# Feed-forward gate and up columns in six pairs of 488, 472, 488, 472, 456 and 440, with the activation made in place

## The reference

```
D_FF = 2816
h = RMSNorm(x)                                 # 256 x 1024
gate, up = split(h @ w_up)                     # w_up is 1024 x 5632: 2816 gate columns, 2816 up columns
x = x + (silu(gate) * up) @ w_down             # w_down is 2816 x 1024
```

## Time and profile before

| | us |
|---|---|
| median of 3 runs | 861.86 (861.78 to 861.89) |
| span of the profiled execution | 859.8 |
| PE busy | 855.7 |
| DVE busy | 593.9 |
| ACT busy | 446.0 |
| POOL busy | 113.6 |

### The profile page before, as it was taken

How to read it: one execution, slowest core, us unless ns; L and a number is a source line. 1 busy time by engine, 2 the same in 40 slices (tenths; PEclk the granted TensorE clock), 3 DMA queues, 4 the chain that set the end, 5 groups by cost and what they waited for, 6 DMA issues and landing times.

```text
span 859.8 us, 11140 instructions
## 1 busy us (share of the span) xinstructions
PE 855.7 (100%) x4246; PEld 711.6 (83%) x4246; DVE 593.9 (69%) x850; ACT 446.0 (52%) x646; POOL 113.6 (13%) x89
## 2 busy tenths in 40 slices
PE   9999999999999999999999999999999999999998
PEld 7888888888888888888888888888888888888887
DVE  7896967768777665564479768768696765565543
ACT  7567654854454444443364674558443644444431
POOL 0750101005401000000005401010063000000000
PEclk9999999999999999999999999999999999999999
DMA  9846656475657666555566465665665576665641
GB/s 343 290 150 190 200 175 183 148 228 180 188 184 236 190 195 190 182 185 189 162 186 178 119 195 158 196 197 162 205 196 179 151 234 183 185 190 177 195 147 50
DMA packets 87815, 160.53 MB, mean 187 GB/s; under 512 B 7505, under 2 KB 14161, under 8 KB 87761
## 3 DMA queue, kind: packets, MB, share of 16 engines
q1 hardware_dynamic: 87328, 159.16, 58.8%
q10 hardware_dynamic: 432, 0.66, 0.2%
HBM read 158.74 MB, written 1.05 MB: 186 GB/s over the span
## 4 chain that ended last, share of the span: by engine, by line
PE 93%; DVE 3%; DMA 2%; ACT 1%; SPq 1%; issue 0%; ACTq 0%
PE bulk L1692 28%; PE bulk L1696 28%; PE bulk L1693 28%; DMA raw<-in_w_in_dram 2%; DVE w_lo L1013 2%; PE bankAB L1432 1%; PE bankAB L1634 1%; PE bankT L1587 0%; PE bankAB L1576 0%; ACT w_hi L737 0%; PE bankAB L1441 0%; PE bankAB L1532 0%; PE bankO L1545 0%; PE bankT L1634 0%; PE bankO L1634 0%
## 5 line engine op out<-in xcount | busy, mean ns | idle before, releaser
L1013 DVE TENSOR_TENSOR w_lo<-raw,w_hi 128x1024 fp32r<-128x1024 f32 (+1 forms) x288 | 362.3, 1272 | 156.5 <-ACT w_hi L737 152.9
L737 ACT ACTIVATE w_hi<-raw 128x1024 fp32r<-128x1024 f32 (+1 forms) x286 | 297.7, 1049 | 245.3 <-PE bulk L1696 240.8
L1692 PE MATMUL bulk<-w_hi,hT_hi 128*128 128x512 f32 (+1 forms) x880 | 344.1, 391 | 0.2 <-DVE w_lo L1013 0.2
L1693 PE MATMUL bulk<-w_lo,hT_hi 128*128 128x512 f32 (+1 forms) x880 | 339.2, 385 | 0.0
L1696 PE MATMUL bulk<-w_hi,hT_lo 128*128 128x512 f32 (+1 forms) x880 | 336.5, 386 | 0.0
L1692 PEld LDWEIGHTS bulk<-w_hi,hT_hi 128*128 128x128 f32 x880 | 165.3, 188 | 33.2 <-DVE w_lo L1013 0.7
L1696 PEld LDWEIGHTS bulk<-w_hi,hT_lo 128*128 128x128 f32 x880 | 165.0, 188 | 33.4
L1693 PEld LDWEIGHTS bulk<-w_lo,hT_hi 128*128 128x128 f32 x880 | 165.4, 188 | 31.7
L1692 PE MATMUL bulk<-w_hi,aT_hi 128*128 128x512 f32 x174 | 68.0, 391 | 0.0
L1696 PE MATMUL bulk<-w_hi,aT_lo 128*128 128x512 f32 x174 | 67.7, 389 | 0.0
L1693 PE MATMUL bulk<-w_lo,aT_hi 128*128 128x512 f32 x174 | 67.7, 389 | 0.0
(11 more groups left out here) (259 smaller groups left out, 720.7 us busy)
## 6 DMA issues: line engine op xcount, KB each, us to landing
raw<-in_w_in_dram SPq DMA_DIRECT2D x110, 512.0 KB, 4.1
raw<-in_w_ffn_up_dram SPq DMA_DIRECT2D x80, 512.0 KB, 4.4
raw<-in_w_ffn_down_dram SPq DMA_DIRECT2D x44, 512.0 KB, 3.3
raw<-in_w_branch_dram SPq DMA_DIRECT2D x20, 512.0 KB, 4.2
raw<-in_w_out_dram SPq DMA_DIRECT2D x16, 512.0 KB, 3.4
bias<-in_b_gate_dram SPq DMA_DIRECT2D x16, 256.0 KB, 4.4
raw<-in_w_ffn_up_dram SPq DMA_DIRECT2D x16, 256.0 KB, 3.2
raw<-in_w_in_dram SPq DMA_DIRECT2D x10, 256.0 KB, 2.7
```

The lines of the kernel that those rows point to most:

```text
L737: act.activation(w_hi[:, g % RING, :, 0:width], raw[:, g % RAW, :, 0:width], ACT.Copy).then_inc(hi_ready, 1)
L1013: vec.tensor_tensor(w_lo[:, g % RING, :, 0:width], raw[:, g % RAW, :, 0:width], w_hi[:, g % RING, :, 0:width].bitcast(F32), ALU.subtract). ...
L1692: pe.matmul(dst, hi, whi, start=(k == ks[0]), stop=False)
L1693: pe.matmul(dst, hi, wlo, start=False, stop=False)
```

## The change

The eleven items become twelve, six pairs of gate and up items with 488, 472, 488, 472, 456 and 440 columns. The mixed item goes. The columns are 5632 as before. Sigmoid, product with the gate and product with the up columns are now all made in one place of `wide`, at column 2048 + `c0 % 1920`. Pairs 4 and 5 wrap round to the start of that row and wait, on ACT, for the transposes of pair `p - 3`; the waits by `p - 2` are gone. Pairs no longer end on multiples of 128, so the transposes of a pair take the blocks that are complete with it: 3, 4, 4, 4, 3 and 4 blocks in place of 4, 4, 4, 4, 4 and 2. A layer has 148 units in place of 144.

```diff
-NPAIR = 5
+FF_WIDTH = (488, 472, 488, 472, 456, 440)
+FF_AT = [sum(FF_WIDTH[:_p]) for _p in range(len(FF_WIDTH) + 1)]
+FF_LAP = 15 * P
+NPAIR = len(FF_WIDTH)
+FF_BLOCKS = [range(FF_AT[_p] // P, FF_AT[_p + 1] // P) for _p in range(NPAIR)]
...
-    ITEMS += [(("ffg", _p), "w_up", [(_p * NC, NC)], KD), (("ffu", _p), "w_up", [(D_FF + _p * NC, NC)], KD)]
-ITEMS += [("fflast", "w_up", [(NPAIR * NC, 256), (D_FF + NPAIR * NC, 256)], KD)]
+    ITEMS += [(("ffg", _p), "w_up", [(FF_AT[_p], FF_WIDTH[_p])], KD), (("ffu", _p), "w_up", [(D_FF + FF_AT[_p], FF_WIDTH[_p])], KD)]
...
-_PE += [(LAST["fflast"] + 3, "tr_act", NPAIR)]
...
-    ffn += [(LAST["fflast"] + 1, "ff_gate", NPAIR), (LAST["fflast"] + 1, "ff_up", NPAIR),
-            (LAST["fflast"] + 3, "act_evac", NPAIR),
-            (U - 3, "residual", "down", 0, 0), (U - 3, "gain", "attn", 0, 0),
+    ffn += [(U - 3, "residual", "down", 0, 0), (U - 3, "gain", "attn", 0, 0),
...
-        def ff_tmp(t, p, width):
-            return wide[:, t, 2048 + 1024 * (p % 2):2048 + 1024 * (p % 2) + width]
-
-        def ff_act(t, p, width):
-            return wide[:, t, 2560 + 1024 * (p % 2):2560 + 1024 * (p % 2) + width]
+        def ff_columns(t, c0, width):
+
+            at = 2048 + c0 % FF_LAP
+            return wide[:, t, at:at + width]
+
+        def ff_act(t, p):
+            return ff_columns(t, FF_AT[p], FF_WIDTH[p])
...
-                    if p >= 2:
-
-                        act.wait_ge(ff_ready, nth(ff_ready, layer, (p - 2, t)))
-                    act.activation(ff_tmp(t, p, width), item_bank(layer, ITEM_AT[item], t)[:, 0:width],
+                    if FF_AT[p] >= FF_LAP:
+
+                        act.wait_ge(stage_done, nth(stage_done, layer, ("tr_act", p - 3, t)))
+                    act.activation(ff_act(t, p), item_bank(layer, ITEM_AT[item], t)[:, 0:width],
...
-                    if p >= 2:
-                        vec.wait_ge(stage_done, nth(stage_done, layer, ("tr_act", p - 2, t)))
-                    vec.scalar_tensor_tensor(out=ff_act(t, p, width), in0=item_bank(layer, ITEM_AT[item], t)[:, c0:c0 + width],
-                                             scalar=y_ffn[:, t:t + 1], in1=ff_tmp(t, p, width), op0=ALU.mult,
+                    vec.scalar_tensor_tensor(out=ff_act(t, p), in0=item_bank(layer, ITEM_AT[item], t)[:, 0:width],
+                                             scalar=y_ffn[:, t:t + 1], in1=ff_act(t, p), op0=ALU.mult,
...
-                    for k in range(blocks):
-                        ins = pe.transpose(bank[name][:, k * P:(k + 1) * P], ff_act(t, p, blocks * P)[:, k * P:(k + 1) * P], identity)
+                    for k, b in enumerate(FF_BLOCKS[p]):
+                        ins = pe.transpose(bank[name][:, k * P:(k + 1) * P], ff_columns(t, b * P, P), identity)
```

More of the change, by code:

```diff
@@ L66 @@
 ITEMS += [(("out", j), "w_out", [(j * NC, NC)], KD) for j in range(2)]
-NPAIR = 5
+FF_WIDTH = (488, 472, 488, 472, 456, 440)
[3 more added lines that the diff above has]
+FF_BLOCKS = [range(FF_AT[_p] // P, FF_AT[_p + 1] // P) for _p in range(NPAIR)]
+FF_PAIR_OF = {_b: _p for _p in range(NPAIR) for _b in FF_BLOCKS[_p]}
+assert FF_AT[NPAIR] == D_FF and FF_LAP in FF_AT and all(len(_b) <= 4 for _b in FF_BLOCKS)
 for _p in range(NPAIR):
-    ITEMS += [(("ffg", _p), "w_up", [(_p * NC, NC)], KD), (("ffu", _p), "w_up", [(D_FF + _p * NC, NC)], KD)]
-ITEMS += [("fflast", "w_up", [(NPAIR * NC, 256), (D_FF + NPAIR * NC, 256)], KD)]
+    ITEMS += [(("ffg", _p), "w_up", [(FF_AT[_p], FF_WIDTH[_p])], KD), (("ffu", _p), "w_up", [(D_FF + FF_AT[_p], FF_WIDTH[_p])], KD)]
 ITEMS += [(("down", j), "w_down", [(j * NC, NC)], KF) for j in range(2)]
@@ L114 @@
 AHEAD = 4
-assert (OFF["gate"] + 8 * NC, U) == (7428, 144)
+assert (OFF["gate"] + 8 * NC, U) == (7428, 148)
 G0 = FIRST[("gate", 0)]
@@ L522, in build @@
         y_ready = {w: signal(f"y_ready_{w}", ["y"]) for w in ("attn", "ffn")}
-        ff_sig = signal("ff_sig", [(p, t) for p in range(NPAIR + 1) for t in range(TT)])
-        ff_gated = signal("ff_gated", [(p, t) for p in range(NPAIR + 1) for t in range(TT)])
-        ff_ready = signal("ff_ready", [(p, t) for p in range(NPAIR + 1) for t in range(TT)])
+        ff_sig = signal("ff_sig", [(p, t) for p in range(NPAIR) for t in range(TT)])
+        ff_gated = signal("ff_gated", [(p, t) for p in range(NPAIR) for t in range(TT)])
+        ff_ready = signal("ff_ready", [(p, t) for p in range(NPAIR) for t in range(TT)])
         def wait_item(engine, layer, name, t):
@@ L540, in released_by @@
                 "out": (x_out, (t, name[1])), "down": (x_down, (t, name[1])),
-                "ffg": (ff_gated, (name[1], t)), "ffu": (ff_ready, (name[1], t)), "fflast": (ff_ready, (NPAIR, t)),
+                "ffg": (ff_gated, (name[1], t)), "ffu": (ff_ready, (name[1], t)),
             }[name if isinstance(name, str) else name[0]]
@@ L925, in ff_gate @@
             def ff_gate(layer, p):
-                item, width = (("ffg", p), NC) if p < NPAIR else ("fflast", 256)
+                item, width = ("ffg", p), FF_WIDTH[p]
                 if p == 0:
@@ L931, in ff_gate @@
                     wait_item(act, layer, item, t)
-                    if p >= 2:
-                        act.wait_ge(ff_ready, nth(ff_ready, layer, (p - 2, t)))
-                    act.activation(ff_tmp(t, p, width), item_bank(layer, ITEM_AT[item], t)[:, 0:width],
+                    if FF_AT[p] >= FF_LAP:
+                        act.wait_ge(stage_done, nth(stage_done, layer, ("tr_act", p - 3, t)))
+                    act.activation(ff_act(t, p), item_bank(layer, ITEM_AT[item], t)[:, 0:width],
                                    ACT.Sigmoid, scale=y_ffn[:, t:t + 1]).then_inc(ff_sig, 1)
             def act_evac(layer, p):
-                blocks = 4 if p < NPAIR else 2
+                blocks = len(FF_BLOCKS[p])
                 for t in range(TT):
                     act.wait_ge(stage_done, nth(stage_done, layer, ("tr_act", p, t)))
-                    lhs_part(layer, ("act", p, t), aT[0][:, 4 * p:4 * p + blocks, t * P:(t + 1) * P],
+                    lhs_part(layer, ("act", p, t), aT[0][:, FF_BLOCKS[p].start:FF_BLOCKS[p].stop, t * P:(t + 1) * P],
                              bank[("AB", "TO")[p % 2][t]][:, 0:blocks * P].rearrange("p (k q) -> p k q", k=blocks))
@@ L1317, in ff_gate @@
             def ff_gate(layer, p):
-                item, width = (("ffg", p), NC) if p < NPAIR else ("fflast", 256)
+                item, width = ("ffg", p), FF_WIDTH[p]
                 for t in range(TT):
                     vec.wait_ge(ff_sig, nth(ff_sig, layer, (p, t)))
-                    s = ff_tmp(t, p, width)
+                    s = ff_act(t, p)
                     vec.scalar_tensor_tensor(out=s, in0=item_bank(layer, ITEM_AT[item], t)[:, 0:width], scalar=y_ffn[:, t:t + 1],
@@ L1326, in ff_up @@
             def ff_up(layer, p):
-                item, c0, width = (("ffu", p), 0, NC) if p < NPAIR else ("fflast", 256, 256)
+                item, width = ("ffu", p), FF_WIDTH[p]
                 for t in range(TT):
@@ L1330, in ff_up @@
                     vec.wait_ge(ff_gated, nth(ff_gated, layer, (p, t)))
-                    if p >= 2:
-                        vec.wait_ge(stage_done, nth(stage_done, layer, ("tr_act", p - 2, t)))
-                    vec.scalar_tensor_tensor(out=ff_act(t, p, width), in0=item_bank(layer, ITEM_AT[item], t)[:, c0:c0 + width],
-                                             scalar=y_ffn[:, t:t + 1], in1=ff_tmp(t, p, width), op0=ALU.mult,
+                    vec.scalar_tensor_tensor(out=ff_act(t, p), in0=item_bank(layer, ITEM_AT[item], t)[:, 0:width],
+                                             scalar=y_ffn[:, t:t + 1], in1=ff_act(t, p), op0=ALU.mult,
                                              op1=ALU.mult).then_inc(ff_ready, 1)
             def act_evac(layer, p):
-                blocks = 4 if p < NPAIR else 2
+                blocks = len(FF_BLOCKS[p])
                 for t in range(TT):
-                    dst = slice(4 * p, 4 * p + blocks)
+                    dst = slice(FF_BLOCKS[p].start, FF_BLOCKS[p].stop)
                     lhs_rest(layer, ("act", p, t), aT[1][:, dst, t * P:(t + 1) * P],
@@ L1647, in lhs_of @@
                 if kind == "down":
-                    return aT, ("act", k // 4, t)
+                    return aT, ("act", FF_PAIR_OF[k], t)
                 if kind == "out":
                     return hT, ("merged", k // 4, t)
-                which = "ffn" if kind in ("ffg", "ffu", "fflast") else "attn"
+                which = "ffn" if kind in ("ffg", "ffu") else "attn"
                 return hT, ("norm", which, t, k // 4)
@@ L1784, in _ @@
                 columns = slice(q * NC // 2, (q + 1) * NC // 2)
-                take("AB"[q], lhs_lo, DEPTH - 1, ("act", NPAIR, 1))
+                take("AB"[q], lhs_lo, DEPTH - 1, ("act", NPAIR - 1, 1))
                 dst = bank["AB"[q]][:, 0:NC // 2]
```

## The result

| | us |
|---|---|
| before, median of 5 runs | 861.85 (861.55 to 861.89) |
| changed kernel, median of 5 runs | 868.64 (868.21 to 868.83) |
| ratio | 1.0079, 95% interval 1.0068 to 1.0090 |
| span of the profiled execution | 867.0 (before 859.8) |

The change makes the kernel slower by 6.8 us, 0.8%. The forecast was 1.9 us faster; the time lies outside the range, beside the third rival's 868.3 us.

What follows compares the result with a forecast made beforehand. PE's matmul starts were taken to bound the kernel: -2.0 us from the w_up matmuls and +0.1 from a wait at F0 gave -1.9 us, so 859.9 us against 861.86, with a range of 855.0 to 863.7.

Steps and rivals of the forecast that it cites:

- third rival: Matmuls of new widths never settle, staying at 17.8 ns over their columns: +6.4 us, 868.3 us; chance 0.15.
- What bounds the kernel: Whole kernel: PE is always busy, so only number and distance of matmul starts, or PE waits (1.5 us before), count.
- The matmuls of w_up: Gate and up columns: 1152 matmuls for 1056, each taken at 10.5 ns over its columns like 260 columns: -2.0 us.
- sign of being wrong: PE's timeline: forecast is wrong if the four widths differ in what they carry, or weight loads set the distance.
- Break-even: Gate and up matmuls: at 12.2 ns over the columns, the 1152 new ones cost the same as the old 1056.
- second rival: Matmuls narrower than a bank carry only 5 to 7 ns over their columns: -7.2 us, about 855 us; chance 0.17.
- Transposes: Feed-forward: still 22 blocks a layer for each tile, six stages and six restarts of some 90 ns: nothing.
- the shorter chain at the end: End of gate and up columns: only the product with the up columns is left, but nobody waited there: nothing.
- in place: Activation in one row: pairs 4 and 5 wait for transposes over 40 us old, hidden behind PE's stream: nothing.
- the split of weights: 48 units a layer for 44: 4 more instructions each on ACT and DVE, 0.35 us more on DVE: nothing.
- loads: w_up loads: 48 DMAs a layer before and after; buffers asked for over 11 us ahead, landing takes 4.4: nothing.
- The start at F0: Each layer's first gate and up matmuls: PE arrives 0.3 us sooner and may wait for `hT_lo`: +0.1 us in all.

Runs made afterwards that it cites:

- the sweep: Kernel before, plus 30 matmuls at each of 42 widths behind its last sum: 512 columns carry 32 cycles over the columns, 260 carry 25, 488 carry 52.
- the last experiment: Kernel before, plus seven widths in eight kinds of matmul behind its last sum: 512 columns read 226.7 ns as the large products are, 215.8 in bfloat16.

## Why the prediction was wrong

- *What bounds the kernel, and that only PE's starts count*: right. The waits of PE stayed under 2 us and the sum over the starts gives the 6.8 us.
- *The matmuls of w_up*: this step failed, in the sentence "I take 10.5 ns". The number was right for 260 columns (24.6 cycles in the sweep), and the reason for carrying it over, that the new widths are no multiples of 16 or 32 either, was false: 272, 288 and 304 columns are multiples of 16 and carry 27 to 29 cycles, near the 25 of 260, while 404 and 472 are none and carry 33 and 40. The runs showed 16.6 to 21.7 ns, 18.6 on average over the 576 matmuls of a layer. 1152 times the 8.1 ns that this is above 10.5 are, but for rounding, the 9.4 us between the forecast of -2.0 and +7.4. The text's own sign of being wrong came true, that the four widths differ among themselves in what they carry. The same term with 13.3 ns would have been 6 us short as well. Break-even was 12.2 ns, as the text had it, and not one of the four widths reaches it.
- *The third rival* had the price nearly right, 17.8 ns and 868.3 us, and its mechanism only in part: 488 and 456 don't settle on one number, as it said, but repeat a pattern with a steady mean, while 472 stands at 512 cycles matmul after matmul and 440 at 480 on average, and both are dear all the same. Its 17.8 ns came from 512 columns on their way to 226.7, which the patterns here are not; that the new widths' mean of 18.6 lies near it is, as far as the runs show, luck. It had a chance of 0.15.
- *The second rival, with the Trainium skill's N / 2.4 + 2.5 ns*: none of the four widths sheds anything. The Trainium skill's rule (TensorE: Matmul & The Clock Gate, Back-to-back issue gap) holds to 0.1 ns in bfloat16 in the last experiment, and fails for float32r by 8 to 19 ns over the widths of the first one.
- *Transposes, the shorter chain at the end, in place, the split of weights, loads*: put at nothing, and the experiment with the old columns in the new structure, +1.1 us for matmuls that should add 1.3, bears it out within its interval of 0.8 us to either side. In the changed kernel itself no wait of PE appeared for any of them. The shorter chain gave no gain, as forecast.
- *The start at F0*: forecast at 0.1 us, not seen. The term was hardly put to the test: it supposed that PE gets there 0.3 us sooner, and at 225.0 ns in place of 213.8 for 488 columns, 24 matmuls gained only 0.04 us. The place in the changed kernel, which answers to the earlier trace rows:

```profile
250.09 2.05 PE L1697 MATMUL bulk<-w_hi,hT_lo 128*128 128x488 f32 x8
251.97 0.39 PE L1693 MATMUL bulk<-w_hi,hT_hi 128*128 128x488 f32 x1
```

  From 250.09 to 251.97 are 1.88 us for eight distances, the restart's (some 0.08 us more) among them, so no wait stands between.
- *Not forecast*: the 0.6 us that came back because the new widths lose less behind restarts.

## What to carry to other kernels

Where PE is the bound, the price of a matmul is its distance from start to start at just that width and type, and it must be read or measured for that width; two neighbours can't be joined by a line. With float32r, 512 columns carry the least over their columns, column for column, of all widths tried here, and cutting them into slightly narrower ones cost 3 to 8 ns a matmul beyond the 13.3 ns of each added one. A shorter chain or one wait less is worth nothing where the chain made nobody wait.

## What the runs showed of the hardware

With float32r operands and a weight load before each matmul, the distance at 2.4 GHz is 32 cycles over the columns for 256, 320 to 384, 400 and 512 columns, 25 to 29 for 260 to 304, and 33 to 52 for all else that was tried between 388 and 508. It repeats with a period of one to some ten matmuls, and at the widths of the kernels it is the same with all other engines idle. In bfloat16, with zeros for data, it is 6 cycles for the seven widths tried from 384 to 512. What makes the rhythm stays open: which bank and which blocks are used plays no part, but for 488 columns with all fixed; the number of stationary columns and the place of the first moving column alter it; the length of the weight load (108 or 188 ns) doesn't set it; and type and data were not told apart.
